# Two feed-forward stages: first row pair without block products, stages joined, token blocks on 64-word places, first slots of the down projection earlier

## The reference, cut to what matters

```python
def _rmsnorm(x, w):
    xf = x.astype(jnp.float32)
    y = xf * lax.rsqrt(jnp.mean(xf * xf, axis=-1, keepdims=True) + EPS)
    return (y * w.astype(jnp.float32)).astype(x.dtype)
def _modulate(x, w, shift, scale):
    return _rmsnorm(x, w) * (1.0 + scale) + shift
def _swiglu(h, w_gate, w_up, w_down):
    return (jax.nn.silu(h @ w_gate) * (h @ w_up)) @ w_down
# end of the first block; the mixers ahead of it are left out
x_new = x + g1 * _merge(y_hg, y_at, gates, w_branch_hgrn[layer], w_branch_attn[layer], w_out[layer])
x_new = x_new + g2 * _swiglu(_modulate(x_new, norm_ffn_w[layer], sh2, sc2),
                             w_ffn_gate[layer], w_ffn_up[layer], w_ffn_down[layer])
# end of the second block
x = x + g1 * y                                  # y = (four mixers) @ w_out
h = rms_norm(x) * (1 + sc2) + sh2
x = x + g2 * ((jax.nn.silu(h @ ffn_w_gate[l]) * (h @ ffn_w_up[l])) @ ffn_w_down[l])
```

## Time and profile before

| what | value |
|---|---|
| median of 3 runs | 3682.88 us (3679.22 to 3700.22) |
| profiled execution | 3701.95 us, span 3700.1 us, mean granted clock 0.931 |
| PE busy | 3355.5 us, 91% of the span |
| DVE, ACT, POOL busy | 1773.1, 1215.6, 602.1 us |
| first network: first pair, 21 pairs, down | 1284.5 to 1340.0, to 1750.7, to 2011.4 us |
| second network: 21 pairs, down | 3015.9 to 3426.6, to 3678.5 us |

### The profile page before, as it was taken

How to read it: one execution, slowest core, us unless ns; L and a number is a source line. 1 busy time by engine, 2 the same in 40 slices (tenths; PEclk the granted TensorE clock), 3 DMA queues, 4 the chain that set the end, 5 groups by cost and what they waited for, 6 DMA issues and landing times. The chain is left out here.

```text
span 3700.1 us, 38241 instructions
## 1 busy us (share of the span) xinstructions
PE 3355.5 (91%) x15144; PEld 2487.0 (67%) x15144; DVE 1773.1 (48%) x2730; ACT 1215.6 (33%) x1851; POOL 602.1 (16%) x588
## 2 busy tenths in 40 slices
PE   7999998897999979999998988988787979999997
PEld 4476544444787768887776776665465858888786
DVE  5547445446233464343764644354755464333344
ACT  2326522222322343332223332442211353333232
POOL 3100000000100054443000010010000044544000
PEclk7999997995999989999999999998898979999998
DMA  5430000000433122222963123233323122222543
GB/s 218 166 125 12 10 34 12 23 1 18 149 102 118 58 86 83 80 86 88 364 256 122 43 78 83 78 114 114 97 88 141 35 100 85 78 83 77 192 149 114
DMA packets 107547, 366.17 MB, mean 99 GB/s; under 512 B 13896, under 2 KB 33352, under 8 KB 89065
## 3 DMA queue, kind: packets, MB, share of 16 engines
q1 hardware_dynamic: 71480, 244.24, 18.7%
q0 software_dynamic: 19232, 111.05, 7.8%
q10 hardware_dynamic: 16656, 8.42, 1.3%
HBM read 300.63 MB, written 63.05 MB: 98 GB/s over the span
## 5 line engine op out<-in xcount | busy, mean ns | idle before, releaser
L2426 PE MATMUL banks<-hidden_high,down_high 128*128 128x512 f32 x704 | 278.0, 395 | 24.0 <-DVE hidden_low L2479 17.9
L2109 POOL TENSOR_TENSOR quad_raw<-quad_raw 128x512 f32<-128x512 f32 x176 | 257.2, 1462 | 241.5 <-DMA quad_raw<-in_w_gu 234.6
L2428 PE MATMUL banks<-hidden_high,down_low 128*128 128x512 f32 x704 | 276.6, 393 | 0.0
L2427 PE MATMUL banks<-hidden_low,down_high 128*128 128x512 f32 x704 | 276.3, 393 | 0.0
L2182 PE MATMUL banks<-block_t_high,quad_low 128*128 128x512 f32 x672 | 266.2, 396 | 0.0
L1584 PE MATMUL banks<-work,weight_ring 128*128 128x512 f32 (+1 forms) x640 | 265.4, 576 | 0.5 <-ACTq L4145 0.5
L1584 PEld LDWEIGHTS banks<-work,weight_ring 128*128 128x128 f32 x640 | 126.8, 201 | 130.3 <-issue 125.0
L2271 ACT ACTIVATE quad_partial<-banks 128x512 f32<-128x512 f32 x176 | 105.0, 598 | 290.9 <-PE banks L2182 279.1
L2182 PE MATMUL banks<-block_b_high,quad_low 128*128 128x512 f32 x504 | 199.5, 396 | 0.0
L2477 DVE TENSOR_TENSOR down_low<-down_raw,down_high 128x2048 fp32r<-128x2048 f32 x44 | 100.8, 2290 | 205.5 <-ACT down_high L2445 205.5
L2181 PE MATMUL banks<-block_t_low,quad_high_b 128*128 128x512 f32 x504 | 198.5, 394 | 0.0
(11 more groups left out here) (587 smaller groups left out, 7424.5 us busy)
## 6 DMA issues: line engine op xcount, KB each, us to landing
down_raw<-in_w_down SPq DMA_DIRECT2D x44, 1024.0 KB, 4.9
quad_raw<-in_w_gu SPq DMA_DIRECT2D x44, 768.0 KB, 4.3
condition_space<-in_mod_w POOLq DMA_DIRECT2D x24, 1024.0 KB, 7.9
ffn_hidden<-quad_gated SPq DMA_DIRECT2D x88, 256.0 KB, 2.0
hidden_raw<-ffn_hidden SPq DMA_DIRECT2D x44, 512.0 KB, 5.9
weight_ring<-in_w_merge SPq DMA_DIRECT2D x24, 512.0 KB, 3.7
weight_ring<-in_dft SPq DMA_DIRECT2D x12, 1024.0 KB, 5.2
quad_raw<-in_w_gu SPq DMA_DIRECT2D x44, 256.0 KB, 3.0
```

The costliest lines, as they stand in the source:

```text
L2109: e.tensor_tensor(self.weight(n, out), self.weight(n, a), self.weight(n, b), op).then_inc(self.sums.sem, 1)
L2426: e.matmul(bank, wh[:, k, m], hh[:, k], start=(p == 0 and k == 0), stop=False)
L2427: e.matmul(bank, wh[:, k, m], hl[:, k], start=False, stop=False)
L2428: mm = e.matmul(bank, wl[:, k, m], hh[:, k], start=False, stop=(p == NP - 1 and k == 1))
```

## The change

Four things change in both networks.

The stages of `linear_split` and `ffn` are joined (`pg.together`), without the barrier.

Pair 0 is computed as four plain products, gate and up by two halves of tokens, 96 matmuls with the token blocks alone. The first 16 of them (`first_matmuls`) are issued at the end of `linear_split`. Pair 1 runs in the order `SECOND_QUAD`, with the last 16 matmuls of pair 0 behind its p1. The step that added the shift to every block (ACT, 16 operations) goes; t2 and t3 get theirs in the bias when their parts are made, in four pieces each. x is stored in two halves from POOL, behind the last evictions of each half.

The area of blocks starts at a multiple of 64 words, with the blocks in another order.

SP issues the loads of down's steps 0, 1 and 2 ahead of the last pair's stores, ACT and DVE make the parts of steps 0 and 1 before the last pair's end, x comes back behind the load of step 7, and the modulation groups lie at other steps.

```diff
-M_END = 53100
+M_END = 53120
...
-            "b11_low", "b21_low", "b11", "b11_high", "b21", "b21_high", "b12", "b22", "t2", "t3", "t1_high", "t2_high", "t3_high", "t4_high"))}
+            "b11_low", "b21_low", "b11_high", "b21_high", "b11", "b21", "t2_high", "t2", "t3_high", "t3", "b22_high", "t4_high", "b12", "b22"))}
...
-        for n, a in enumerate((M_RING, M_F + 4096, M_F + 4096 + 6144)):
+        for n, a in enumerate((M_RING, at["b11_low"], at["t2_high"])):
...
+        squares.ahead.first_matmuls(e)
...
+SECOND_QUAD = ("p1", "p2", "p6", "p7", "p5", "p4", "p3")
+FIRST_PRODUCTS = {"gate_1": 1, "up_1": 2, "gate_2": 4, "up_2": 5}, {"p1": 3}
...
+    def first_matmuls(self, e):
+        e.wait_ge(self.pg.ps_free, self.f0 - 3)
+        self.w_low.wait(e, 1)
+        self.first_high(e, 0, 0, 4)
...
+        if n == 1:
+            self.x_stored.wait(e, 32)
+            self.scaled.wait(e, KT + 2)
+        else:
+            self.products.wait(e, self.done(n - 2, "p2" if n > 2 else "up_2"))
+            if n > 2:
+                self.sums.wait(e, 4 * (n - 3) + 4)
+        e.dma_start(raw[:, 0:3 * HALF], self.w[n][:, 0:3 * HALF]).then_inc(self.landed_x[n % 2].sem, 16)
+
...
+    def first_high(self, e, s, a, b):
+
+        for k in range(a, b):
+            self.rounded.wait(e, KT * s + k + 1)
+            for up, w_hi, w_lo in self.first_operands(k):
+                bank = self.first_bank(up, s)
+                e.matmul(bank, w_hi, self.block_part(s, k, "high"), start=(k == 0), stop=False)
+                e.matmul(bank, w_lo, self.block_part(s, k, "high"), start=False, stop=False)
+
+    def first_lows(self, e, s):
+
+        for k in range(KT):
+            self.split.wait(e, KT * s + k + 1)
+            for up, w_hi, _ in self.first_operands(k):
+                mm = e.matmul(self.first_bank(up, s), w_hi, self.block_part(s, k, "low"), start=False, stop=(k == KT - 1))
+                if k == KT - 1:
+                    mm.then_inc(self.products.sem, 1)
+
...
-                before_last(e)
+                for i in range(3):
+                    down_load(e, i)
...
-        self.sum_s3(e, 0)
-        self.sums_s124(e, 0)
-        e.wait_ge(pg.stage_done, 3 * self.k_at)
-        e.dma_start(x_kept, pg.x).then_inc(self.x_stored.sem, 16)
-        self.whole.wait(e, 4 + KT)
-        e.tensor_tensor(pg.b_raw["t3"], pg.b_raw["b22"], pg.b_raw["b12"], ALU.subtract).then_inc(self.third.sem, 1)
+        for s in range(2):
+            half = slice(s * HALF, (s + 1) * HALF)
+            e.wait_ge(pg.ps_free, self.f0 - 2 * (1 - s))
+            e.dma_start(self.x_kept[:, :, half], pg.x[:, :, half]).then_inc(self.x_stored.sem, 16)
         self.sum_s3(e, 1)
...
+        self.sums_s124(e, 1)
+        self.sum_s3(e, 2)
...
-        for n in range(FT):
+        self.w_low.wait(e, 2)
+        self.first_high(e, 0, 4, KT)
+        self.first_lows(e, 0)
+        self.first_high(e, 1, 0, KT)
+        self.w_low.wait(e, 3)
+        self.pe_product(e, 1, "p1")
+        self.first_lows(e, 1)
+        for product in SECOND_QUAD[1:]:
+            self.pe_product(e, 1, product)
...
-        self.shift_blocks(e, 1, 0, KT)
-        self.shift_blocks(e, 0, 4, KT)
...
+        self.round_blocks(e, 1, 0, KT)
+        self.products.wait(e, self.done(0, "gate_1"))
+        e.activation(pg.gated[:, 2, :], self.first_bank(0, 0), ACT.Silu).then_inc(self.silu_1.sem, 1)
+        self.weights_high(e, 1, 0)
+        self.block_high(e, "t2")
+        self.weights_high(e, 1, 1)
+        self.block_high(e, "t3")
+        self.products.wait(e, self.done(0, "gate_2"))
+        e.activation(pg.gated[:, 3, :], self.first_bank(0, 1), ACT.Silu).then_inc(self.silu_2.sem, 1)
+        self.block_high(e, "t1")
+        self.block_high(e, "t4")
 
...
+            else:
+                down_high(e, 0)
...
+        down_high(e, 1)
         silu_2(FT - 1)
...
+        for k in range(4):
+            e.tensor_tensor(self.shift_change[:, k:k + 1], self.shift(4 + k), self.shift(k), ALU.subtract)
+        self.low_blocks(e, 0, 0, KT)
         self.scale_blocks(e, 1, 0, KT)
...
         e.tensor_tensor(raw["t1"], raw["b12"], raw["b11"], ALU.subtract).then_inc(self.turned.sem, 1)
...
         e.tensor_tensor(raw["t2"], raw["b22"], raw["t1"], ALU.subtract).then_inc(self.turned.sem, 1)
...
+        e.tensor_tensor(raw["t3"], raw["b22"], raw["b12"], ALU.subtract).then_inc(self.turned.sem, 1)
+        self.weights_low(e, 1, 0)
+        self.turned.wait(e, 3)
+        self.low_blocks(e, 1, 0, 4)
         e.tensor_tensor(raw["t4"], raw["b21"], raw["t2"], ALU.subtract).then_inc(self.turned.sem, 1)
...
+        self.low_blocks(e, 1, 4, KT)
+        self.products.wait(e, self.done(0, "up_1"))
+        self.silu_1.wait(e, 1)
+        e.tensor_tensor(f[:, 2, :], f[:, 2, :], self.first_bank(1, 0), ALU.mult).then_inc(self.out[0].sem, 1)
...
+        self.weights_low(e, 1, 1)
+        self.turned.wait(e, 4)
+        self.block_low(e, 0, "t2")
+        self.block_low(e, 1, "t3")
...
-        two_of = {n: (2 * i, 2 * i + 1) for i, n in enumerate((1, 2, 3, 4, 5, 6, 7, 8, 9, 10, 14, 15))}
+        groups_of = {n: (i,) for i, n in enumerate((2, 3, 4, 5, 6, 9, 10, 11))}
+        groups_of.update({n: (8 + 2 * i, 9 + 2 * i) for i, n in enumerate(range(13, 21))})
...
+    last_read = (quad.done(FT - 2, "p3"), quad.done(FT - 1, "p2"), quad.done(FT - 1, "p7"))
...
-                quad.products.wait(e, all_used if n else all_used - 7)
+                quad.products.wait(e, last_read[n])
...
-        quad.sync(e, lambda e: load(e, 0))
-        for n in range(1, NS):
+        quad.sync(e, lambda e, n: load(e, n))
+        for n in range(3, NS):
             load(e, n)
-            if n == 2:
+            if n == 7:
                 e.dma_start(x, x_kept).then_inc(x_back.sem, 16)
...
+        quad.scalar(e, parts_high)
...
+    pg.together(name, 2)
```

More of the change, by code:

```diff
@@ L2021, in __init__ @@
         self.roots = Roots(pg, self.squares, self.rs)
[L2022 removed]
+        self.f0 = pg.fill
+        self.shift_change = pg.perm_left(4)
         s = lambda n, c: pg.shared_sem(f"quad_{n}", c)
[L2024 to L2026 removed]
+        self.scaled, self.rounded, self.split = s("scaled", 2 * KT), s("first_high", 2 * KT), s("first_low", 2 * KT)
@@ L2027, in __init__ @@
+        self.turned, self.high, self.low = s("blocks", 4), s("block_high", 4), s("block_low", 4)
+        self.landed_x = [s(f"weights_x_{n}", 16 * (FT // 2 + (n == 0))) for n in range(2)]
         self.landed_y = [s(f"weights_y_{n}", 16 * FT // 2) for n in range(2)]
-        self.sums, self.w_high, self.w_low = s("weight_sums", 4 * FT), s("weight_high", 2 * FT), s("weight_low", 2 * FT)
-        self.products, self.copied, self.joined = s("products", 7 * FT), s("copied", 4 * FT), s("joined", 3 * FT)
@@ L2076, in shift_blocks @@
-    def shift_blocks(self, e, s, a, b):
-        for k in range(a, b):
-            if s == 0:
-                self.first_low.wait(e, k + 1)
-            else:
-                self.scaled.wait(e, KT + k + 1)
-            v = self.block(s, k)
-            e.activation(v, v, ACT.Identity, bias=self.shift(k)).then_inc(self.whole.sem, 1)
+            self.rounded.wait(e, KT * s + k + 1)
+            e.scalar_tensor_tensor(out=self.block_part(s, k, "low"), in0=self.block(s, k), scalar=self.shift(k),
+                                   in1=self.block_part(s, k, "high").bitcast(F32), op0=ALU.add,
+                                   op1=ALU.subtract).then_inc(self.split.sem, 1)
@@ L2249, in scalar, with block_high @@
-    def scalar(self, e):
+                self.pe_product(e, n, product)
+    def block_high(self, e, name):
+        pg = self.pg
+        raw, high = pg.b_raw[name], pg.b_parts[name + "_high"]
+        self.turned.wait(e, int(name[1]))
+        if name in ("t1", "t4"):
+            self.products.wait(e, self.done(0, "up_2"))
+            e.activation(high, raw, ACT.Copy).then_inc(self.high.sem, 1)
+            return
+        for k in range(4):
+            bias = self.shift(4 + k) if name == "t2" else self.shift_change[:, k:k + 1]
+            op = e.activation(high[:, k, :], raw[:, k, :], ACT.Identity, bias=bias)
+        op.then_inc(self.high.sem, 1)
@@ new lines, in block_low @@
+    def block_low(self, e, i, name):
+        pg = self.pg
+        raw, high, low = pg.b_raw[name], pg.b_parts[name + "_high"], pg.b_parts[name + "_low"]
+        self.high.wait(e, i + 1)
+        if name in ("t1", "t4"):
+            e.tensor_tensor(low, raw, high.bitcast(F32), ALU.subtract).then_inc(self.low.sem, 1)
+            return
+        for k in range(4):
+            shift = self.shift(4 + k) if name == "t2" else self.shift_change[:, k:k + 1]
+            op = e.scalar_tensor_tensor(out=low[:, k, :], in0=raw[:, k, :], scalar=shift, in1=high[:, k, :].bitcast(F32),
+                                        op0=ALU.add, op1=ALU.subtract)
+        op.then_inc(self.low.sem, 1)
@@ L2251, in scalar @@
+    def scalar(self, e, down_high):
```

(13 more changed lines are left out.)

276 lines of the change are left out of this document (140 added, 136 removed).

## The result

| | before | changed |
|---|---|---|
| median (range, runs) | 3690.58 (3679.22 to 3700.22, 4) | 3635.61 (3623.67 to 3639.06, 4) |
| ratio to before | | 0.984, interval 0.9813 to 0.9866 |
| same kernels again (`control`) | 3694.86 (11 runs) | 3628.52 (5 runs), ratio 0.9828 (0.9806 to 0.9849) |
| profiled execution, span | 3701.95, 3700.1 | 3633.1, 3631.2 |
| mean granted clock | 0.931 | 0.940 |

A forecast was written before the change was run, and what follows sets the result against it. PE was taken as the bound: the latest operand at the start, matmul count and distance in the pairs. Terms 19.4 + 19.1 + 23.0 + 3.5 = 65.0 us off the median 3682.88 gave 3618 us; own range 3605 to 3632, with rivals 3600 to 3638.

The forecast's parts named there:

- an entry that gives little: Rival: two new PE waits at pair 1's weights and pair 2's reload eat the entry gain; about 3635 us, chance 0.13.
- a place that gives nothing: Rival: something else in the pairs, such as loads or POOL's sums, sets their distance; 3637 us, chance 0.10.
- the rivals at its edges: Place gives nothing (3637 us, 0.10), entry gives little (about 3635, 0.13), entry gives more (3600, 0.07).
- the low end of the entry: Entry gain if POOL's sums and the reload cost their dearer price, 3.3 us each twice: 2.6 us.
- entry, both networks: From the projection to pair 2: pair 2 starts at 1349.9 instead of 1359.63, 9.7 us per network, 19.4 for both.
- place of the blocks: Pairs 1 to 21: blocks at a multiple of 64 words give down's 227.0 ns per matmul; 19.1 us for both networks.
- start of down: Gap before down step 0 and its slow clock go, through early loads and parts: 13.46 and 9.53 us, 23.0 in all.
- middle of down: Step 11's wait for DVE in the first network shrinks with fewer modulation groups at steps 9 to 12; 3.5 us.
- two PE waits near 9 us: Idle PE before pair 1's p1 (9.6 us, its weights) and p2 (about 9 us, copy behind pair 2's high parts).
- the dearer of the two prices: POOL's sum S3 for pair 2: 1.3 us alone, 3.3 us when taking turns with DVE.
- the 1 us that the prediction allowed: Last pair: p4 waits for p7's copy behind ACT's parts of down step 0; at most 1 us if late.
- The slow rival: Stores of x in 2 KB pieces take 35 us a half, delaying pair 1's load 48 us per network; 3714 us, chance 0.02.

The follow-up runs named there:

- copies_first: Changed kernel with ACT copying the banks of pair 1's p1 and p6 before making high parts of pair 2's first weights; ratio to before 0.9790.
- place_alone: Kernel before with only the token blocks moved to a multiple of 64 words (M_END 53100 to 53120); ratio to before 0.9946.
- place_undone: Changed kernel with the token blocks again 48 words behind a multiple of 64; ratio to before 0.9871.
- down_late: Changed kernel with down's loads 1 and 2 and parts of steps 0 and 1 back behind the last pair; ratio to before 0.9872.
- groups_back: Changed kernel with the modulation groups at the steps of before, x still coming back behind step 7; ratio to before 0.9860.
- p1_early: As copies_first, with the copy of pair 1's p1 also ahead of ACT's high parts of t1 and t4; ratio to before 0.9820.
- store_whole: Changed kernel with x stored by one 4 MB transfer behind the last eviction instead of two halves; ratio to before 0.9843.

## Why the prediction was right, and where it was off

The change acts through the four terms that were forecast, each at its place. The total alone would not have shown it: 3635.61 is 17.6 us above the forecast, lies outside the prediction's own range of 3605 to 3632, and is nearer to what two of its rivals said (3635 for an entry that gives little, 3637 for a place that gives nothing). It lies within 3600 to 3638 because that range takes in the rivals at its edges. The prediction's own range doesn't follow from its ends either: they give 3607 to 3636, and the low end of the entry is 2.6 us a network in one place (9.7 less twice 3.3 is 3.1) and 10 for both in the other. What decides is the terms, measured in the two profiles by starts of matmuls:

| term | forecast | measured | how |
|---|---|---|---|
| entry, both networks | 19.4 | 17.1 | 75.5 - 66.9 = 8.6 and 75.5 - 66.9 = 8.5 |
| place of the blocks | 19.1 | 19.5 | pair 2 to last matmul: 390.69, twice, against 381.13 and 380.78 |
| start of down | 23.0 | 23.0 | last pair matmul to step 1: 24.59 and 20.66 against 11.11 |
| middle of down | 3.5 | 4.8 | steps 10 and 11 of the first network: 28.32 to 23.52 |
| sum | 65.0 | 64.4 | whole stretch, projection's end to down's end: 36.8 + 28.4 = 65.1 |

The 0.7 us between the sum and the whole are down's other steps, which take 10.88 us instead of 10.90.

**Entry.** The picture of two PE waits near 9 us was right: 9.2 and 10.5. POOL's four sums took 10.89 us (11.2 forecast), shown below. What was mis-sized is the second wait, 10.5 where 9 were taken: POOL's first sum for pair 2 came at the dearer of the two prices in the working (3.5 us from its start to that of ACT's part), and it started 5.0 us behind the issue of its load where 4.3 were taken. `copies_first` showed that this wait was the order on ACT only in part, 5 of the 10 us. POOL's four sums of pair 1 and PE's first wait, in the changed kernel:

```profile
1294.89 10.89 POOL L2142 TENSOR_TENSOR quad_raw<-quad_raw 128x512 f32<-128x512 f32 x4 [12.91 <-DMA quad_raw<-in_w_gu]
...
1307.70 0.80 PE L2254 MATMUL banks<-block_b_high,quad_high_a 128*128 128x512 f32 x1 [9.23 <-DVE quad_low L2196]
```

**Place.** `place_alone` and `place_undone` show this term with one constant, both ways, and the rival that place gives nothing is out. Twenty pairs give 10.1 us a network (390.69 to 380.57 in `place_alone`); the changed kernel loses 0.6 and 0.2 of them in the last pair. In the first network p4 waits there for its copy, which stands behind ACT's parts for down, within the 1 us that the prediction allowed. The prediction took "PE and ACT never wait on anyone" in the Trainium skill, "SBUF — State Buffer", section "Who interferes with whom", to mean that a place changes nothing. Read so, it doesn't hold here: PE's distance rises from 226.7 to 232.7 ns when its data lie 48 words off. Why was not tried: whether weights and data of PE meet in one resource, or another engine or a transfer has a part in it, is open.

**Start of down.** The size was exact, which was partly luck: the early loads and parts give 18 of 23 us (`down_late`), and the prediction credited all of it to them. Of the rest, 4.3 us were the modulation's first operation on ACT, which the prediction did not see.

**Middle.** Mis-sized by 1.3 us: the wait fell by 3.1 as forecast, but step 11 itself also went from 12.60 to 10.97 us, where only a little was taken for the slow clock. That x may come back five loads later for nothing was right only together with the new table (`groups_back`).

**The base.** The terms were right, and the step that was off in the final number is the last one: "so I take 65 off the median: 3618 us". The median of three runs, 3682.88, was low; it was 3690.58 with a fourth and 3694.86 over 11 later ones, and 65 off the profiled 3701.95 is 3637, beside 3633.1 of the changed kernel's profile. The difference of the two profiled times is 68.9, 3.8 more than the two networks give; the rest lies in stretches that the change does not touch. The windows from 48 to 70 us, far ahead of the change, of the kernel before, the changed one and `copies_first`:

```profile
48.00:70.00 22.00, 22.00 (x57) 14.55 (x57) 15.57 (x20) 5.34 (x8) 9.05 (x6) 0.50 0.14 49
```

```profile
48.00:70.00 22.00, 22.00 (x68) 13.63 (x68) 18.98 (x26) 6.62 (x10) 9.97 (x6) 0.66 0.14 49
```

```profile
48.00:70.00 22.00, 22.00 (x75) 14.05 (x76) 15.65 (x21) 5.34 (x8) 9.71 (x6) 0.90 0.14 49
```

The same code ran there at a mean granted clock of 0.50, 0.66 or 0.90, and by the last matmul of the first network's projection executions differ by up to 11 us (1275 to 1287 in all profiles). This stretch is one example and not the whole cause: `p1_early` had 0.66 there too, as the changed kernel, and was at 1286.56 where that was at 1279.06. The 31 executions of the kernel before lie between 3679.22 and 3708.88, with a standard deviation of 5.9 us; from them I estimate that a median of three places a forecast no better than within some 8 us.

**The slow rival.** `store_whole` and the landing of the halves in 7.5 to 9.1 us settle it: below the price of the whole store, and not 35. The fit in the Trainium skill, "DMA: Bandwidth & Descriptors", section "Anatomy of one DMA — SWDGE (gpsimd) path", gives an estimate of 6.8 us for such a half; the measured 7.5 to 9.1 decide.

## What to carry to other kernels

When a wait is removed, list what stands behind it in the same engine's queue: here three operations on ACT took turns as the one that held PE, and each further fix showed a part of the gain or none. Look in it also for an operation that waits for something unrelated in front of one that is needed, as the modulation's first did here. Compare the distance of matmul starts between loops of the same form; a difference of 2.6% with no idle time was worth 20 us, and the place of the operands in SBUF set it. Work out a forecast against the profile's own time, and give the base its own uncertainty when it comes from few runs.

## What the runs showed of the hardware that was not expected

With the weights of the slots at multiples of 64 words, the distance of 128x128 by 128x512 fp32r matmuls is 226.7 ns with data at a multiple of 64, 229.6 at 16 words behind one, 232.1 at 32 and 232.7 at 48 (pair distance / 84; part of the even pairs' weights moves with the data). Idle time of like length did not cost the same: after 9.2 us idle before pair 1, `copies_first` was at full clock by the end of p1 and `p1_early`, with the same idle time, some three us later. The windows of PE from p1 on show mean clocks of 0.82 and 0.67:

```profile
1304.90:1313.10 8.20, 8.12 (x28) 6.03 (x28) 8.20 (x12) 2.63 (x6) 0.00 (x0) 0.82 0.00 0
```

```profile
1315.10:1324.60 9.50, 9.41 (x29) 7.55 (x30) 9.50 (x12) 3.24 (x7) 0.00 (x0) 0.67 0.00 0
```

That is 1.3 us of `p1_early`'s loss against `copies_first`, and comes from no wait.
